# Pausing weight loads for DMA transposes, a by-token convolution mixer, and two 512-token tiles in a four-layer decoder trunk

## The chip, the cores and the metric

The kernel runs on the 8 cores of one Trainium2 chip, the same program on each, with no exchange between them. Each core has TensorE (PE) for matrix multiplies, whose results go to PSUM (8 banks of 512 float32 columns), VectorE (DVE), ScalarE (ACT), GpSimd (POOL) and SyncE (SP), the last two of which issue most transfers. The metric is the device time of the slowest core in microseconds (us).

## The reference, cut to what matters

Every core computes one prompt of 2048 tokens and 64 sample tokens through four layers. A layer is: a half-step SwiGLU feed-forward (FFN), a token mixer, and a second half-step FFN, each between two RMS norms.

```python
for i in range(4):
    f = swiglu(rmsnorm(h, g[0]), ffn_w_in[i, 0], ffn_w_down[i, 0])   # 1024 -> 2 x 2816 -> 1024
    h = h + 0.5 * rmsnorm(f, g[1])
    xm = rmsnorm(h, g[2])
    m = (conformer_conv, short_gated_conv, chunk_gmlp, multiscale_pool)[i](xm, ...)
    h = h + rmsnorm(m, g[3])
    f = swiglu(rmsnorm(h, g[4]), ffn_w_in[i, 1], ffn_w_down[i, 1])
    h = h + 0.5 * rmsnorm(f, g[5])
```

Mixer a (`conformer_conv`) projects to 2 x 1024 channels, gates (GLU), convolves each channel causally over 31 tokens, applies LayerNorm and swish, and projects out. Mixer b is a gated convolution of width 3, mixer c a chunked gMLP with GELU, a LayerNorm and a 128 x 128 position mixing, mixer d a causal pooling. Matrices are bfloat16 on TensorE, sums float32.

## The kernel before, in words

**A planner writes the program.** `build_program` runs generators (one for each chain of work) against a small model of the engines (`Prog`, `Sched`). Whenever its model of PE is free, `Sched.run` takes the ready request (`Pe`) with the smallest priority tuple and appends its matmuls to PE's stream; the other engines' streams grow the same way. The order on every engine is thus fixed at build time, and the chip keeps it whatever the real durations are. Semaphore waits are added for every true dependency.

**Work is tiled by tokens.** Two groups (`NG = 2`) pass one after the other through 11 stages each: group 0 has prompt tokens 0 to 1023 and the 64 sample tokens, group 1 has tokens 1024 to 2047. Stage number k counts 0 to 21; an FFN is one stage, a mixer one (mixer d is part of the chain after an FFN). A group's tokens are 8 `Tok` of 128 (taus 0 to 7; tau 8 is the samples). For matmuls whose moving operand is activations, they form three `NTile` of 384, 384 and 256 tokens (320 in group 0, with the samples).

**An FFN stage.** `ffn_in` multiplies, for each of 22 column blocks j of 128, gate and up: 8 matmuls (kc) each of a stationary 128x128 weight block against `xn[:, kc, nt.sl]`, for every NTile, in the order (q, jj, tile, gate/up) with j = 2q + jj. ACT evaluates Silu of the gate into a buffer `sg` (pool `P_SG`), DVE multiplies it with the up bank into `gb`. `ffn_down` (by `tok_mm`) multiplies tau by tau: 44 matmuls of 512 columns for a full tau, 11 weight slots (kb) in turn, all eleven needed by each tau.

**After each tau's last product** runs `chain`: `post` (square sum on ACT, power on POOL, two wide DVE operations) and `pre` (the same again for the next norm, one wide DVE operation into `xmb`, 3 buffers), and then the tau must be transposed into `xn`, channels on partitions, for stage k + 1. `pre` has two ways. By DMA: one transposing transfer on SP's queue. By PE: 8 transposes (line 84) into a bank and one copy out, on ACT as a rule. The DMA way is taken where `via == 'dma'` and the planner's model of POOL's queue would be empty within `LIGHT` = 4.0 us. That model takes 5 us for each weight load. Mixer a's chains say 'pe'; those of mixers b and c and of the FFNs say 'dma', and so fall to PE wherever the modelled queue is longer. The sample tau always goes by PE.

**Weights** stream through a ring of 16 slots of 4 KB per partition in one planned order (`build_plan`). `w_pump` issues the next load on POOL's queue as soon as a slot is free; a slot is freed (`w_free`) when every token tile has used it. Some slots are only lent as scratch ('lent': W, C, F for mixer a), with no load.

**Mixer a** (`mixer_a`): the in-projection has 8 channel blocks c, each for 3 NTiles, priority `(k, q // 2, nt.idx, c)`: c 0 to 3 for all tokens, then c 4 to 7 for all tokens. The convolution works on items (ct, hf): 256 tokens by four channel blocks, half hf, listed with all four hf = 0 items first. Each item first needs a shifted copy of its inputs in a buffer `xr` (2 buffers): `xr_load` issues 8 transfers on SP (16 for each of the 4 sample items of group 0) and makes 8 DVE copies. Then 128 matmuls with 32 stationary columns follow at priority `(k, -2, ...)`, ahead of everything else of the stage. When both halves of a ct are done, `stats` sums, normalises (DVE) and applies swish (ACT) into `xn`; then the out-projection of its taus, priority `(k, -1, ...)`, may run. The F slots hold the convolution's float32 results: six are lent, so hf = 0 items have their own slot each and hf = 1 items share two. The next FFN starts (`nextlane`) when the last main item is convolved, and goes beyond its column block 6 only when the sample items are done too.

**Mixer b** ends its in-projection with q = 3 and then has an out-projection of 8 (9) taus of 16 matmuls. **Mixer c** has v products tau by tau, u products by NTile, a position mixing (`splane`), and such an out-projection.

The ends of lines that readers of the profile meet: line 83 is any matmul, 84 a PE transpose, 85 an ACT activation, 86 to 89 DVE and POOL arithmetic, 242 any DMA issue.

Of the kernel before, what the change touches and what calls it, by code (L numbers as in the profile page):

```python
# [354 lines left out]


class Banks:
    def __init__(self, p):
# [171 lines left out]
def build_plan():  # L530
# [64 lines left out]
def build_program():  # L595
# [37 lines left out]
    with contextlib.ExitStack() as st:  # L633
# [47 lines left out]
        SG0 = A.reserve(4608)  # L681
        sg = [A.at(SG0 + i * 1536, [384], F32) for i in range(3)]
        h = A.alloc([9, D], F32)
# [8 lines left out]
        exts = A.at(o, [8, 34, 16], BF16); o += 8 * 34 * 16 * 2  # L692
        XR0 = o
        xr = [A.at(o + i * 16 * NXR * 2, [4, 4, NXR], BF16) for i in range(2)]
        xrs = [A.at(o + i * 16 * NXR * 2, [4, 2, 512], BF16) for i in range(2)]
        xrz = [A.at(o + i * 16 * NXR * 2, [8 * NXR], F32) for i in range(2)]
        o += 2 * 16 * NXR * 2
        glus2 = A.at(o, [8, NS], F32); o += 8 * NS * 4
        glus = A.at(o, [8, NS], F32); o += 8 * NS * 4
        gluf = A.at(XR0 - 8704, [8, 32], F32)  # L700
        assert o <= G0 + GSZ, (o - G0, GSZ)
# [19 lines left out]
        P_XMB = Pool(S, 'xmb', 3)  # L721
        P_SG = Pool(S, 'sg', 3)
        P_ZB = Pool(S, 'zb', 3)
# [3 lines left out]
        def grab(pool):  # L727
            while not pool.free:
                yield pool
            return pool.take()  # L730

        plan = []
# [7 lines left out]
        class WS:  # L740
            nxt = 0
            free = list(range(RING))
            slot = {}
            cap = 0

        def slot_off(k):
# [255 lines left out]
        def ffn_in(k, g_, l, s, nts, gate=None):  # L1002
            done = [Count(len(nts), lambda q=q: w_free((g_, 'fi', l, s, q, 0), (g_, 'fi', l, s, q, 1))) for q in range(NQ)]

            def ev(nt, j, up, bg, tg):
                n = nt.n
                yield p.t(tg)
                i = yield from grab(P_SG)
                ps, pid = bk(bg)
# [60 lines left out]
        def ffn_down(k, g_, l, s, taus, spawn):  # L1070
            yield from tok_mm(k, taus, lambda kc, t: gb[:, kc, t.sl],
                              lambda kb, t: [('g', k, t.n, 2 * kb), ('g', k, t.n, 2 * kb + 1)],
                              lambda kb, t: [('g', t.n, 2 * kb), ('g', t.n, 2 * kb + 1)],
                              [(g_, 'fd', l, s, kb) for kb in range(NQ)], NJ, spawn)

        XRI = [('xr', i, e) for i in range(2) for e in 'dv']

        def mixer_a(k, g_, nts, taus, nextlane):
            new = [('glub', n, c) for n in range(3) for c in range(8)] + ['glub_h', 'glub_p', 'exts_st', 'gluf'] + XRI + \
                  [(nm, c) for nm in ('exts', 'glus2', 'glus') for c in range(8)]  # L1080
            p.inherit(new, G_ALL)
            smp = g_ == 0
            last = g_ == NG - 1

            def init():
# [35 lines left out]
            def ev(c, nt, bg, tg):  # L1121
                n, np_ = nt.n, nt.npr
                yield p.t(tg)
                i = yield from grab(P_SG)
                ps, pid = bk(bg)
# [31 lines left out]
            def sub(nt):  # L1157
                n = nt.n
                for q in range(4):
                    kv, kg = (g_, 'ai', q, 0), (g_, 'ai', q, 1)  # L1160
                    for jj in range(2):
                        c = 2 * q + jj

                        def mm(b, key):
# [30 lines left out]
            NCT = GP // CT  # L1195
            items = [(ct, 0, None) for ct in range(NCT)] + [(ct, 1, None) for ct in range(NCT)]
            if smp:
                items += [('s', i // 2, i) for i in range(4)]

            def xr_load(i):  # L1200
                ct, hf, si = items[i]
                b = i % 2
                if ct == 's':
# [10 lines left out]
                else:  # L1214
# [14 lines left out]
                if i >= 2:  # L1229
                    yield Flag(('xfree', k, i - 2))  # L1230
                    yield p.rt_w([('xr', b, 'd'), ('xr', b, 'v')])
# [24 lines left out]
            def conv():  # L1256
                for i, (ct, hf, si) in enumerate(items):
                    n = CT if ct != 's' else NS
                    first = ct != 's' or si % 2 == 0
                    x = i % 2  # L1260
                    if ct != 's':
# [6 lines left out]
                    if first:  # L1268
                        fkey = 0 if ct == 's' else ct if hf == 0 else 4 + ct % 2
                        ids = [('fb', ct, c) for c in range(4 * hf, 4 * hf + 4)]  # L1270
                        if ct == 's':
                            p.inherit(ids, [('glus2', c) for c in range(4 * hf, 4 * hf + 4)])
                            off = None
                        elif hf == 1 and ct >= 2:
                            yield Flag(('lnd', k, ct - 2))
                            p.inherit(ids, [('fb', ct - 2, c) for c in range(4, 8)])
                            off = slot_off(PIDX[(g_, 'F', fkey)])
# [139 lines left out]
            def fclose(i):  # L1417
                yield Flag(('lnd', k, i))
                lent_close((g_, 'F', i), [('fb', i, c) for c in range(4)])
                if i >= 2:  # L1420
                    lent_close((g_, 'F', 2 + i), [('fb', ct, c) for ct in (i - 2, i) for c in range(4, 8)])
            for i in range(NCT):
                S.spawn(fclose(i))
# [8 lines left out]
        def mixer_b(k, g_, nts, taus, nextlane):  # L1432
# [13 lines left out]
            def ev(c, nt, b, tok):  # L1446
                n, np_ = nt.n, nt.npr
                yield p.t(tok)
                i = yield from grab(P_ZB)
                i2 = yield from grab(P_SG)  # L1450
                zk = zb[i]
# [46 lines left out]
            def sub(nt):  # L1498
                n = nt.n
                for q in range(4):  # L1500
                    for jj in range(2):
                        c = 2 * q + jj
                        for part, nm in ((2, 'bX'), (1, 'bC'), (0, 'bB')):
# [38 lines left out]
        def mixer_c(k, g_, nts, taus, nextlane):  # L1542
# [87 lines left out]
            def vlane(nt):  # L1630
                for t in nt.taus:
                    P = t.P
                    bb = None
                    for kb in range(4):
# [16 lines left out]
                        vcnt[kb].hit()  # L1651
                    S.spawn(v_ev(t, bb, tok))
                S.set(('vd', k, nt.idx))

            def sev(nt, hh, b, tok):
                n, np_ = nt.n, nt.npr
                yield p.t(tok)
                i = yield from grab(P_SG)
                ps, bid = bk(b)
# [49 lines left out]
            def after():  # L1709
                for nt in nts:  # L1710
                    yield Flag(('spd', k, nt.idx))
                if smp:
# [289 lines left out]
        for g_ in range(NG):  # L2002
            taus = [Tok(i, 128, i // 3 if i < 6 else 2) for i in range(8)]
            if g_ == 0:
                taus.append(Tok(8, 64, 2))
            nts = [NTile(0, 0, 384, 0, taus[0:3]), NTile(1, 384, 384, 0, taus[3:6]),
                   NTile(2, 768, 256, NS if g_ == 0 else 0, taus[6:])]
            groups.append((taus, nts))
        NSTG = 11
# [7 lines left out]
        def start(k, gate=None):  # L2017
            if k >= NSTG * NG:
                return
            g_, i = k // NSTG, k % NSTG  # L2020
            taus, nts = groups[g_]
            kind, l, s = KINDS[i]
# [123 lines left out]
```

How the kernel before makes its waits and increments, by code:

```python
    def _emit_waits(self, eng, deps):  # L158
        for sk in sorted(deps, key=str):
            v = deps[sk]
            if sk == ('e', eng) and eng in ('pe', 'sp'):
                continue
            if self.waited[eng].get(sk, 0) >= v:
                continue
            self.waited[eng][sk] = v
            sem = self.semh[sk]
            self.streams[eng].append(lambda e, sem=sem, v=v: e.wait_ge(sem, v))
# [37 lines left out]
    def op(self, eng, fns, reads=(), writes=(), cost=None):  # L205
        writes = list(writes) + [b for b in reads if isinstance(b, tuple) and b[0] == 'ps']
        deps = self._deps(reads, writes)
        self._emit_waits(eng, deps)
        if isinstance(fns, Fn):
            fns = [fns]
        if cost is None:
            cost = sum(f.cost(eng) for f in fns)
        start = self._start(eng, deps)
        self.efree[eng] = start + cost
        self.busy[eng] += cost
        self.ecount[eng] += 1
        c = self.ecount[eng]
        sem = self.semh[('e', eng)]
        for f in fns[:-1]:
            self.streams[eng].append(f)
        last = fns[-1]
        self.streams[eng].append(lambda e, last=last, sem=sem: last(e).then_inc(sem, 1))
        tok = (('e', eng), c)
        self.tend[tok] = start + cost + (0.17 if eng == 'pe' else 0.03)
        self._record(tok, reads, writes)
        return tok
```

## Time and profile before

| | us |
|---|---|
| median of 3 runs | 4662.27 (4657.13 to 4664.70) |
| the profiled execution, its own time | 4654.91 |
| its span, slowest core | 4653.4 (cores 4644.1 to 4653.4) |
| PE busy | 4566.7, 98% |
| DVE / ACT / POOL busy | 1770.4 / 1281.3 / 608.6 |
| share of PE in the chain that ended last | 92% |

The profile is one execution. Its page gives each engine's busy time and the costliest groups; a group is one line, engine and operation with its operands, the count behind an x, the busy time of the whole group, the mean duration of one instruction in ns, and the idle time of its engine ahead of it with what ended that. Matmuls overlap (a 384-column one is shown as 326 ns but the next starts 163 ns after it), so their pace is read from start to start. PEclk is the granted TensorE clock as a share of 2.4 GHz.

### The profile page before, as it was taken

The numbers are of one execution on the slowest core, as the hardware profiler recorded it, in microseconds if no ns is written. First come the engines' busy times: TensorE is split into PE (matmuls) and PEld (weight loads), VectorE is DVE, ScalarE is ACT, GpSimd is POOL, SyncE is SP. The second block draws the span as 40 slices with busy tenths as digits, with TensorE's granted clock in tenths as the row PEclk, the third lists the DMA queues.
The fourth block names the chain that finished last, engine by engine and source line by source line (L and its number), as shares of the span: only waits on it lengthen the run. The fifth ranks groups of instructions, "written<-read, shape, count | busy, mean of one in ns | idle before, by whom it ended". The sixth has DMA issues, their size and how long they took to land.

```text
span 4653.4 us, 83035 instructions; the slowest of 8 cores (4644.1 to 4653.4 us)
## 1 busy us (share of the span) xinstructions
PE 4566.7 (98%) x30474; PEld 2698.2 (58%) x30474; DVE 1770.4 (38%) x3156; ACT 1281.3 (28%) x2499; POOL 608.6 (13%) x1102
## 2 busy tenths in 40 slices
PE   7998999999999999999999989999999999999999
PEld 4555656556555565565646566565665655656564
DVE  2366232373232542326232472323723236232622
ACT  2135222233221331224121252222322225121421
POOL 1112110011010110102010111101101012010210
PEclk9998999999999999999999999999999999999999
DMA  8336527264263543635565246363543636444361
GB/s 167 68 73 124 103 53 137 48 117 85 55 111 62 106 84 61 118 60 93 98 139 98 63 90 112 57 118 57 105 92 57 117 57 123 73 80 98 60 119 41
DMA packets 228042, 416.39 MB, mean 89 GB/s; under 512 B 114095, under 2 KB 136879, under 8 KB 227630
## 3 DMA queue, kind: packets, MB, share of 16 engines
q0 software_dynamic: 88592, 319.79, 39.6%
q1 hardware_dynamic: 139054, 91.30, 8.0%
q8 instruction: 251, 4.11, 0.4%
q14 instruction: 145, 1.19, 0.1%
HBM read 682.92 MB, written 12.71 MB: 149 GB/s over the span
## 4 chain that ended last, share of the span: by engine, by line
PE 92%; DVE 2%; issue 2%; DMA 2%; SPq 1%; ACT 1%; POOL 0%; DVEq 0%; ACTq 0%; POOLq 0%
PE ps L83 91%; DVE big L88 1%; SPq L242 1%; PE ps L84 1%; ACT big L85 1%; DVE big L86 1%; DMA big<-wst 1%; DMA big<-big 1%; DMA big<-xp 0%; DVE big L89 0%; POOL big L86 0%; DVE big L87 0%; DVEq L167 0%; POOL big L242 0%; ACTq L167 0%
## 5 line engine op out<-in xcount | busy, mean ns | idle before, releaser
L83 PE MATMUL ps<-big 128*128 128x384 bf16 (+5 forms) x29758 | 4535.4, 322 | 47.6 <-DMA big<-big 13.3
L83 PEld LDWEIGHTS ps<-big 128*128 128x128 bf16 (+1 forms) x29758 | 2653.9, 99 | 1897.5 <-issue 137.4
L85 ACT ACTIVATE big<-ps 128x384 f32<-128x384 f32 (+5 forms) x1526 | 875.4, 577 | 2829.1 <-PE ps L83 2721.3
L86 DVE TENSOR_TENSOR big<-ps,big 128x384 bf16<-128x384 f32 (+6 forms) x1386 | 856.6, 618 | 1855.6 <-PE ps L83 1838.0
L88 DVE SCALAR_TENSOR_TENSOR big<-big 128x1024 bf16<-128x1024 f32 (+9 forms) x591 | 585.4, 995 | 184.0 <-POOL big L86 115.8
L242 POOL DMA_DIRECT2D big<-wst x608 | 327.2, 542 | 2456.3 <-PE ps L83 2296.4
L85 ACT ACTIVATE big<-big 128x1024 bf16<-128x1024 f32 (+5 forms) x454 | 344.4, 774 | 480.8 <-DVE big L88 308.7
L86 POOL TENSOR_TENSOR big<-big 128x1 f32<-128x1 f32 (+1 forms) x434 | 261.8, 605 | 1537.7 <-DVE big L87 1313.8
L87 DVE TENSOR_SCALAR big<-big 128x1 f32<-128x1 f32 (+2 forms) x439 | 78.6, 180 | 716.7 <-ACT big L85 703.2
L89 DVE COPY big<-big 32x1136 bf16<-32x1136 bf16 (+4 forms) x281 | 81.7, 291 | 19.5 <-ACT big L85 7.8
L84 PE MATMUL ps<-big 128*128 128x128 bf16 x716 | 57.5, 224 | 29.3 <-DVE big L88 18.1
L86 DVE TENSOR_TENSOR big<-big 128x384 bf16<-128x384 f32 (+13 forms) x120 | 78.9, 666 | 17.0 <-POOL big L91 9.3
L84 PEld LDWEIGHTS ps<-big 128*128 128x128 bf16 x716 | 47.8, 100 | 47.5 <-issue 37.9
L85 ACT ACTIVATE big<-ps,big 128x256 bf16<-128x256 f32 (+1 forms) x72 | 32.4, 453 | 45.6 <-PE ps L83 44.1
L87 DVE TENSOR_SCALAR big<-ps,big 128x256 f32<-128x256 f32 (+1 forms) x72 | 32.3, 459 | 32.7 <-ACT big L85 31.9
L85 ACT ACTIVATION_READ_ACCUMULATOR big<-ps 128x1 f32 x221 | 43.4, 196 | 0.0
L86 DVE TENSOR_TENSOR big<-big,ps 128x1024 f32<-128x1024 f32 (+1 forms) x36 | 40.6, 1129 | 2.9 <-PE ps L83 0.8
L85 ACT ACTIVATION_READ_ACCUMULATOR big<-big 128x1 f32 (+1 forms) x221 | 41.6, 188 | 0.0
L88 DVE SCALAR_TENSOR_TENSOR big<-ps,big 128x384 f32<-128x384 f32 (+2 forms) x64 | 31.2, 506 | 18.0 <-PE ps L83 13.1
L88 DVE SCALAR_TENSOR_TENSOR big<-big,ps 128x384 bf16<-128x384 f32 (+1 forms) x64 | 27.4, 432 | 25.0 <-PE ps L83 22.6
L91 POOL TENSOR_SCALAR_AFFINE_SELECT big<-big 128x64 bf16<-128x64 bf16 (+7 forms) x50 | 12.5, 257 | 42.4 <-DVE big L90 15.5
L85 ACT ACT_TABLE_LOAD x5 | 6.4, 1283 | 8.1 <-DMA big<-xp 5.9
(9 smaller groups left out, 20.5 us busy)
## 6 DMA issues: line engine op xcount, KB each, us to landing
big<-wst POOLq DMA_DIRECT2D x608, 512.0 KB, 8.4
big<-gains SPq DMA_DIRECT2D x52, 512.0 KB, 10.6
big<-xp SPq DMA_DIRECT2D x16, 512.0 KB, 5.1
yp<-big SPq DMA_DIRECT2D x16, 512.0 KB, 4.1
big<-big SPq DMA_DIRECT2D x64, 71.0 KB, 2.5
big<-big SPq DMA_DIRECT2D x64, 70.8 KB, 2.7
big<-big SPq DMA_DIRECT2D x48, 64.0 KB, 2.3
big<-dwx SPq DMA_DIRECT2D x4, 512.0 KB, 4.3
```

The lines of the kernel that those rows point to most:

```text
L83: 'matmul': lambda e, *a, **k: e.matmul(*a, **k),
L84: 'transpose': lambda e, *a, **k: e.transpose(*a, **k),
L85: 'activation': lambda e, *a, **k: e.activation(*a, **k),
L86: 'tensor_tensor': lambda e, *a, **k: e.tensor_tensor(*a, **k),
L87: 'tensor_scalar': lambda e, *a, **k: e.tensor_scalar(*a, **k),
L88: 'scalar_tensor_tensor': lambda e, *a, **k: e.scalar_tensor_tensor(*a, **k),
L89: 'tensor_copy': lambda e, *a, **k: e.tensor_copy(*a, **k),
L91: 'affine_select': lambda e, *a, **k: e.affine_select(*a, **k),
L242: self.streams[q].append(lambda e, out=out, in_=in_, sem=sem: e.dma_start(out=out, in_=in_).then_inc(sem, 16))
```

## The change

Three edits, in the diff below, in the order of its parts.

1. **The mixer a stage goes by tokens.** In-projection priority `(k, nt.idx, c, 0)`; items listed (ct 0, hf 0), (ct 0, hf 1), (ct 1, hf 0) and so on; three `xr` buffers in group 1 (the third lies where group 0 has its sample state), two in group 0; four F slots instead of six, of which ct 2 and 3 take those of ct 0 and 1 after these are normalised; the lent slots are planned after all eight in-projection loads instead of amid them; DVE copies of `xr_load` step back while DVE is busy (`polite`).
2. **Weight loads pause.** `w_hold(flag)` stops `w_pump` until a flag is set. Mixer b calls it after its last in-projection request, mixer c after its last v request; the flag is the last tau's `xn` for stage k + 1. Mixer c's chains say 'pe' for taus 0 to 2 and 'dma' for the others.
3. **Two tiles of 512 tokens** for `ffn_in` in group 1, in place of 384 + 384 + 256. The Silu buffers become two of 512 columns or three of 384 in the same bytes (`Widths`). Mixers keep three tiles.

```diff
+class Widths(Pool):
+    CLASH = {0: (3,), 1: (3, 4), 2: (4,), 3: (0, 1), 4: (1, 2)}
+    def take(self, wide):
+        c = [i for i in ((3, 4) if wide else (0, 1, 2)) if i not in self.busy and not any(x in self.busy for x in self.CLASH[i])]
...
-                        if q == 1:
-                            for i in range(4):
-                                lend(('W', i))
-                            for i in range(2):
-                                lend(('C', i))
-                            lend(('F', 0))
-                            lend(('F', 1))
-                    for i in range(2, 6):
+                    for i in range(2):
+                        lend(('W', 2 * i))
+                        lend(('W', 2 * i + 1))
+                        lend(('C', i))
+                        lend(('F', i))
+                    for i in range(2, 4):
                         lend(('F', i))
...
-            while WS.nxt < min(len(plan), WS.cap) and WS.free:
+            while WS.nxt < min(len(plan), WS.cap) and WS.free and not WS.held:
...
+        def w_hold(flag):
+            def rel():
+                yield Flag(flag)
+                WS.held = False
+                w_pump()
+            WS.held = True
+            S.spawn(rel())
...
-                for i in range(2):
+                for i in range(NX):
                     yield S.now + 1.0
                     p.op('pool', I.memset(xrz[i], 0.0), writes=[('xr', i, 'd'), ('xr', i, 'v')])
...
-                        pr = (k, q // 2, nt.idx, c)
+                        pr = (k, nt.idx, c, 0)
...
-            items = [(ct, 0, None) for ct in range(NCT)] + [(ct, 1, None) for ct in range(NCT)]
+            items = [(ct, hf, None) for ct in range(NCT) for hf in range(2)]
...
+                        yield from polite()
                         t2 = p.op('dve', fns, reads=rd, writes=[('xr', b, 'v')], cost=0.9)
...
-                        fkey = 0 if ct == 's' else ct if hf == 0 else 4 + ct % 2
+                        fkey = 0 if ct == 's' else 2 * (ct % 2) + hf
...
-                        elif hf == 1 and ct >= 2:
+                        elif ct >= 2:
                             yield Flag(('lnd', k, ct - 2))
...
+                    if q == 3 and nt is nts[-1]:
+                        w_hold(('xn', k + 1, taus[-1].idx))
...
+                    if t is taus[-1]:
+                        w_hold(('xn', k + 1, taus[-1].idx))
...
-                              [(g_, 'co', kb) for kb in range(4)], 8, lambda t, b: chain(k, t, b, False))
+                              [(g_, 'co', kb) for kb in range(4)], 8, lambda t, b: chain(k, t, b, False, 'pe' if t.idx < 3 else 'dma'))
...
+            ntf = nts
+            if g_ > 0:
+                ntf = [NTile(0, 0, 512, 0, taus[0:4]), NTile(1, 512, 512, 0, taus[4:8])]
...
-            ffn_in(k, g_, l, s, nts, gate)
+            ffn_in(k, g_, l, s, ntf, gate)
```

## Rows read from the trace of the kernel before

**Rows 1.** Page of the profile: engines' busy time, then the last chain by engine.

```profile
PE 4566.7 (98%) x30474; PEld 2698.2 (58%) x30474; DVE 1770.4 (38%) x3156; ACT 1281.3 (28%) x2499; POOL 608.6 (13%) x1102
...
PE 92%; DVE 2%; issue 2%; DMA 2%; SPq 1%; ACT 1%; POOL 0%; DVEq 0%; ACTq 0%; POOLq 0%
```

**Rows 2.** Stretches: us, busy of PE, PEld, DVE, ACT, POOL, PEclk, DMA share, GB/s.

```profile
280.80:364.80 84.00, 82.67 (x1130) 57.48 (x1132) 62.93 (x136) 34.58 (x89) 9.83 (x12) 1.00 0.51 95
364.80:470.00 105.20, 83.31 (x1071) 49.91 (x1071) 69.46 (x127) 58.66 (x128) 23.88 (x38) 0.87 0.73 133
...
2650.00:2736.80 86.80, 83.19 (x1249) 60.46 (x1247) 62.57 (x131) 33.80 (x78) 9.47 (x8) 1.00 0.44 96
2736.80:2801.00 64.20, 55.52 (x563) 33.40 (x563) 52.41 (x83) 44.44 (x85) 21.54 (x33) 0.92 0.65 112
```

**Rows 3.** PE in order of time, start, us, count, idle: stage 13's end to 14's.

```profile
3022.98 10.13 PE L83 MATMUL ps<-big 128*128 128x512 bf16 x60
...
3033.39 221.08 PE L83 MATMUL ps<-big 128*128 128x384 bf16 x1348
3254.31 0.61 PE L84 MATMUL ps<-big 128*128 128x128 bf16 x8
```

**Rows 4.** PE in order of time, end of mixer c in group 1.

```profile
3909.69 3.62 PE L83 MATMUL ps<-big 128*128 128x512 bf16 x16
3913.14 0.61 PE L84 MATMUL ps<-big 128*128 128x128 bf16 x8
3913.59 3.62 PE L83 MATMUL ps<-big 128*128 128x512 bf16 x16
...
3931.43 4.06 PE L83 MATMUL ps<-big 128*128 128x384 bf16 x24
3935.33 0.61 PE L84 MATMUL ps<-big 128*128 128x128 bf16 x8
```

**Rows 5.** Groups by form, 3030 to 3178: busy us, mean ns, idle before.

```profile
L83 PEld LDWEIGHTS ps<-big 128*128 128x128 bf16 x1008 | 97.1, 98 | 50.4 <-issue 3.9
L86 DVE TENSOR_TENSOR big<-ps,big 128x384 bf16<-128x384 f32 x42 | 23.4, 557 | 86.8 <-PE ps L83 86.8
L85 ACT ACTIVATE big<-ps 128x384 f32<-128x384 f32 x42 | 20.6, 491 | 82.8 <-PE ps L83 82.8
```

**Rows 6.** Groups by form, 3183 to 3252 (down-projection), weight loads of PE.

```profile
L83 PEld LDWEIGHTS ps<-big 128*128 128x128 bf16 x320 | 31.3, 98 | 37.8
```

**Rows 7.** Line 84 alone, from mixer b's and c's out-projections to the last transpose.

```profile
1030.00:1078.00 48.00, 4.65 (x60) 3.93 (x60) 1.00 0.55 95
1618.00:1673.00 55.00, 5.27 (x68) 4.47 (x68) 1.00 0.59 115
3342.00:3386.00 44.00, 4.87 (x64) 4.05 (x64) 1.00 0.50 101
3897.00:3943.00 46.00, 4.88 (x64) 4.18 (x64) 1.00 0.66 126
```

**Rows 8.** DMA issues of the page: count, KB each, median us to landing.

```profile
big<-wst POOLq DMA_DIRECT2D x608, 512.0 KB, 8.4
...
big<-big SPq DMA_TRANSPOSE x92, 3.1
```

**Rows 9.** POOL in order of time around mixer c's out-projection in group 1.

```profile
3888.59 0.53 POOL L242 DMA_DIRECT2D big<-wst  x1 [0.29 <-issue]
...
3925.68 1.10 POOL L242 DMA_DIRECT2D big<-wst  x2
```

**Rows 10.** GB/s in 40 slices of 3342 to 3386 (1.1 us each).

```profile
GB/s 0 15 67 186 220 201 216 201 223 123 0 0 0 0 0 0 7 7 0 0 0 0 0 0 0 15 0 0 134 175 175 186 227 194 223 272 276 283 216 190
```

**Rows 11.** What PE waited for, 364 to 470: us, times, longest.

```profile
PE ps L83 <- DMA big<-big: 13.3, 4, 6.6
```

**Rows 12.** SP's queue in order of time, 350 to 450: start, us, what.

```profile
356.02 11.47 SPq L242 DMA_DIRECT2D big<-big  x16
```

**Rows 13.** The chain that ended last, 364 to 470: start, us, what.

```profile
366.85 16.73 DMA big<-big
```

More of the change, by code:

```diff
@@ L354, in give, with __init__ @@
             self.S.push(self.S.now, self.waiters.pop(0))
+class Widths(Pool):
+    CLASH = {0: (3,), 1: (3, 4), 2: (4,), 3: (0, 1), 4: (1, 2)}
+    def __init__(self, S, name):
+        Pool.__init__(self, S, name, 0)
+        self.busy = set()
+    def take(self, wide):
+        c = [i for i in ((3, 4) if wide else (0, 1, 2)) if i not in self.busy and not any(x in self.busy for x in self.CLASH[i])]
+        if not c:
+            return None
+        k = min(c, key=lambda i: self.S.p.rt_w([(self.name, x) for x in (i,) + self.CLASH[i]]))
+        self.S.p.inherit([(self.name, k)], [(self.name, x) for x in self.CLASH[k]])
+        self.busy.add(k)
+        return k
+    def give(self, k):
+        self.busy.remove(k)
+        w, self.waiters = self.waiters, []
+        for g in w:
+            self.S.push(self.S.now, g)
 class Banks:
@@ L681, in build_program @@
         SG0 = A.reserve(4608)
-        sg = [A.at(SG0 + i * 1536, [384], F32) for i in range(3)]
+        sg = [A.at(SG0 + i * 1536, [384], F32) for i in range(3)] + [A.at(SG0 + i * 2560, [512], F32) for i in range(2)]
         h = A.alloc([9, D], F32)
@@ L692, in build_program @@
         exts = A.at(o, [8, 34, 16], BF16); o += 8 * 34 * 16 * 2
[L693 to L697, printed above, removed]
         glus2 = A.at(o, [8, NS], F32); o += 8 * NS * 4
         glus = A.at(o, [8, NS], F32); o += 8 * NS * 4
-        gluf = A.at(XR0 - 8704, [8, 32], F32)
+        gluf = A.at(o - 1024, [8, 32], F32)
+        XRO = [o, o + 32 * NXR, G0 + 8 * (32 + GP) * 2]
+        assert XRO[2] + 32 * NXR <= o - 1024
+        xr = [A.at(x, [4, 4, NXR], BF16) for x in XRO]
+        xrs = [A.at(x, [4, 2, 512], BF16) for x in XRO]
+        xrz = [A.at(x, [8 * NXR], F32) for x in XRO]
+        o += 2 * 32 * NXR
         assert o <= G0 + GSZ, (o - G0, GSZ)
@@ L721, in build_program @@
         P_XMB = Pool(S, 'xmb', 3)
-        P_SG = Pool(S, 'sg', 3)
+        P_SG = Widths(S, 'sg')
         P_ZB = Pool(S, 'zb', 3)
@@ L730, in grab, with polite, grab_sg @@
             return pool.take()
+        def polite(eng='dve'):
+            while p.efree[eng] > S.now + 0.25:
+                yield p.efree[eng] - 0.15
+        def grab_sg(n):
+            while True:
+                k = P_SG.take(n > 384)
+                if k is not None:
+                    return k
+                yield P_SG
         plan = []
@@ L744, in build_program @@
             cap = 0
+            held = False
         def slot_off(k):
@@ L1007, in ev @@
                 yield p.t(tg)
-                i = yield from grab(P_SG)
+                i = yield from grab_sg(n)
                 ps, pid = bk(bg)
@@ L1071, in ffn_down @@
             yield from tok_mm(k, taus, lambda kc, t: gb[:, kc, t.sl],
-                              lambda kb, t: [('g', k, t.n, 2 * kb), ('g', k, t.n, 2 * kb + 1)],
-                              lambda kb, t: [('g', t.n, 2 * kb), ('g', t.n, 2 * kb + 1)],
+                              lambda kb, t: [('g', k, t.nf, 2 * kb), ('g', k, t.nf, 2 * kb + 1)],
+                              lambda kb, t: [('g', t.nf, 2 * kb), ('g', t.nf, 2 * kb + 1)],
                               [(g_, 'fd', l, s, kb) for kb in range(NQ)], NJ, spawn)
-        XRI = [('xr', i, e) for i in range(2) for e in 'dv']
+        XRI = [('xr', i, e) for i in range(3) for e in 'dv']
         def mixer_a(k, g_, nts, taus, nextlane):
@@ L1082, in mixer_a @@
             smp = g_ == 0
+            NX = 2 if smp else 3
             last = g_ == NG - 1
@@ L1123, in ev @@
                 yield p.t(tg)
-                i = yield from grab(P_SG)
+                i = yield from grab_sg(n)
                 ps, pid = bk(bg)
@@ L1201, in xr_load @@
                 ct, hf, si = items[i]
-                b = i % 2
+                b = i % NX
                 if ct == 's':
@@ L1228, in piece @@
                                 glub[32 * q:32 * q + 32, 4 * hf:4 * hf + 4, t0 + s_:t0 + s_ + w])
-                if i >= 2:
-                    yield Flag(('xfree', k, i - 2))
+                if i >= NX:
+                    yield Flag(('xfree', k, i - NX))
                     yield p.rt_w([('xr', b, 'd'), ('xr', b, 'v')])
@@ L1259, in conv @@
                     first = ct != 's' or si % 2 == 0
-                    x = i % 2
+                    x = i % NX
                     if ct != 's':
@@ L1273, in conv @@
                             off = None
-                        elif hf == 1 and ct >= 2:
+                        elif ct >= 2:
                             yield Flag(('lnd', k, ct - 2))
-                            p.inherit(ids, [('fb', ct - 2, c) for c in range(4, 8)])
+                            p.inherit(ids, [('fb', ct - 2, c) for c in range(4 * hf, 4 * hf + 4)])
                             off = slot_off(PIDX[(g_, 'F', fkey)])
@@ L1418, in fclose @@
                 yield Flag(('lnd', k, i))
[L1419 to L1422, printed above, removed]
+                for hf in range(2):
+                    lent_close((g_, 'F', 2 * (i % 2) + hf), [('fb', ct, c) for ct in (i - 2, i) for c in range(4 * hf, 4 * hf + 4)])
+            for i in range(2, NCT):
                 S.spawn(fclose(i))
@@ L1449, in ev @@
                 i = yield from grab(P_ZB)
-                i2 = yield from grab(P_SG)
+                i2 = yield from grab_sg(n)
                 zk = zb[i]
@@ L1657, in sev @@
                 yield p.t(tok)
-                i = yield from grab(P_SG)
+                i = yield from grab_sg(n)
                 ps, bid = bk(b)
@@ L2007, in build_program @@
                    NTile(2, 768, 256, NS if g_ == 0 else 0, taus[6:])]
-            groups.append((taus, nts))
+            ntf = nts
+            if g_ > 0:
+                ntf = [NTile(0, 0, 512, 0, taus[0:4]), NTile(1, 512, 512, 0, taus[4:8])]
+            for n in ntf:
+                for t in n.taus:
+                    t.nf = n.idx
+            groups.append((taus, nts, ntf))
         NSTG = 11
@@ L2020, in start @@
             g_, i = k // NSTG, k % NSTG
-            taus, nts = groups[g_]
+            taus, nts, ntf = groups[g_]
             kind, l, s = KINDS[i]
```

## The prediction

> **What bounds the kernel now.** I read the page first: PE is busy 98% of the span and makes up 92% of the chain that ended last, DVE 38%, ACT 28% [rows 1]. So time can only come from three places: PE's idle time (4653.4 - 4566.7 = 87 us), stretches at half clock, and matmul time itself. Next I read the table of stretches, to see where the first two lie. Both mixer a stages stand out [rows 2]. Group 0 spends 189.2 us there with PE idle 1.3 + 21.9 = 23.2 us, and a granted clock of 0.87 over 105.2 us, which is 13.7 us of lost clock; group 1 spends 151 us with 3.6 + 8.7 = 12.3 us idle and 0.08 x 64.2 = 5.1 us of lost clock. Together 54 us. The clock is at its upper level (2.4 GHz) before PE begins to wait and falls to the lower one within the waits. Third, I read PE in order of time, start to start, for the pace of each form. A run of 16 down-projection matmuls of 512 columns takes 3.45 us, 0.2156 us each; 24 matmuls of 384 columns take 3.90 us, 0.1625 us each; 8 transposes 0.45 us [rows 4].
>
> **Part 3, two tiles of 512.** Between two transposes lie 221 us without a gap: 3033.39 to 3254.31 is 220.92 us for 1348 matmuls [rows 3]. The run of 60 matmuls at 3022.98 begins with the last 4 of stage 13's down-projection, so 56 of stage 14's 1056 in-projection matmuls (704 of 384 columns, 352 of 256) are in it, all of 384. The long run thus has 648 of 384, 352 of 256 and 348 of 512 columns. 348 x 0.2156 = 75.0 and 648 x 0.1625 = 105.3, so the 352 small ones cost 40.6 us, 0.115 us each, where 256 columns at 2.4 GHz are 0.107 us. The in-projection costs 105.3 + 9.1 (the 56) + 40.6 = 155.0 us; with 704 matmuls of 512 columns it costs 704 x 0.2156 = 151.8 us. The saving is 3.2 us in each of 8 FFN stages of group 1: **25 us**.
>
> Where it comes from matters, since a fixed cost for each matmul would not give so much. The weight loads of the in-projection show 3.9 us of idle time put down to "issue" in 148 us; in the down-projection none [rows 5, 6]. I read it so: at a change of bank PE's queue holds a semaphore wait ahead of the next weight load (98 ns), and a 256-column matmul is too short to cover both, one of 512 is not. It is about once per block j. The lower end: the wait stays visible behind 512 columns and only the rest of the difference remains, 25 - 8 x 22 x 0.1 = 8 us. The upper end is the 25.
>
> The Trainium skill (TensorE: Matmul & The Clock Gate, "Wait — 56ns, not 53.3ns?") gives the warm start-to-start time as N / 2.4 GHz plus about 2.5 ns. By that rule alone three tiles made two save one such cost in 352 x 8 places, an estimate of 7 us in place of 25. The trace agrees with it for 384 and 512 columns and not for 256.
>
> Other engines: Silu of 384 columns is 491 ns and the product 557 ns [rows 5]; by proportion 512 columns are at most 655 and 743 ns. A gate and up pair then takes PE 3.45 us, and an `sg` buffer is held from the gate's end to the product's, about 1.73 + 0.9 = 2.6 us. Two buffers suffice; DVE is a third busy. At a stage's start tile 0 now needs tau 3 too. In the FFN after mixer c the transposes of taus 0 to 3 come during the last four out-projection taus, so tau 3 may be late by its landing, 1 to 2 us; where an FFN or a mixer b went before, it is early. I take 0, range 0 to 5 us for all. Tile 0 alone has 76 us of products to cover the chains of taus 4 to 7.
>
> **Part 2, the pause.** Transposes by PE around the four out-projections of mixers b and c: 60, 68, 64 and 64, in 4.9 us or so each [rows 7]. That is 7 full taus and the half-size sample tau (4), then 8 and that, 8, 8. A DMA transpose lands in 3.1 us [rows 8]. The choice hangs on the planner's queue: at mixer b's tau 0 it still holds the loads that the last in-projection block frees, 3 x 5 us modelled; the pause leaves these out, and the queue falls under 4 us. I expect 7 + 8 taus of mixer b and taus 3 to 7 of mixer c twice: 25 taus, 25 x 0.45 = **11 us** of PE, and 25 copies of ACT. Lower end 3 us (mixer c's five of one group and little else), upper end 14 us (with small waits of PE ahead of transposes). The latency is about equal: 3.1 us against 0.45 plus a copy plus the wait for a slot on PE.
>
> What queues behind the pause is POOL's weight loads. In group 1 the loads of 3888 and on, which mixer c's v and u slots free, and those of 3925 [rows 9] all wait for tau 7's `xn` at about 3942. At that point at least 4 slots hold q 0 and 1 of the next FFN, probably 6. Tile 0 alone uses q 0 and 1 in 13.8 us from 3927, so PE has work until 3941, then tile 1 becomes ready and has the same again until 3955. Real loads under a backlog move 190 to 230 GB/s [rows 10], 2.3 to 2.8 us for a slot of 0.52 MB; q 2 lands by 3950. I take 0; 0 to 3 us for each mixer c, nothing for mixer b, whose ring holds about nine slots of the next FFN. The debt of ten slots is repaid at 2.8 us a slot against a use of 6.9.
>
> **Part 1, mixer a by tokens.** The matmuls stay. What changes is what is ready when PE would wait. Now, after the last in-projection product (364.8 and 2736.8), five (in group 1 six) of eight main items are convolved, and the rest, LayerNorm and all eight out-projection taus hang on one another. PE waited 13.3 us for `xr` transfers in group 0, longest 6.6 [rows 11]; the transfer before the next item took 16.7 us, among five weight loads [rows 13], where an item's 8 issues take 8 x 11.47 / 16 = 5.7 us of SP [rows 12]. By tokens, ct 0 is done a third through the projection and its LayerNorm and two out-projection taus fit under the rest. Against it: eight in-projection weights and eight lent slots fill the ring of 16, and the weights are freed only by the last token tile. So F 2 and 3, and with them ct 1, wait for c 1 of tile 2, and `ao` for c 3 to 5. From there (T) SP needs for group 1's items 5 to 7, with three buffers, about 25 us; PE has 10.5 us of in-projection, six items of 3.7 us (22 us) and two ready out-projection taus (7 us): 39 us. So the transfers are covered. After item 7 LayerNorm takes about 15 us, against which stand four out-projection taus (14 us) and the next FFN's first tile. I expect group 1 to keep 4 of 12 us of idle and 2 of 5 of clock: -11. In group 0 SP needs about 31 us for items 4 to 7 and then 4 x 11.5 = 46 us for the sample items, unchanged by the order, and cover runs out there as now. Of the 37 us there I take 7 off. Sum **-18 us**. Bounds: -45 (nearly all of 54 gone), and +15 (the tail of out-projections is used up early, and PE waits for 17 us landings once more in each group).
>
> **Sum.** 25 + 11 + 18 = 54 us less; I add 3 for the small waits above: -51 us, so 4654.9 - 51 = 4604 for an execution like the profiled one. The median of the runs shown is 7.4 us above that execution: 4662.3 - 51 = **4611 us**.
>
> **Rivals.** (a) Mixer a gains nothing: what the tail saves by being shorter it loses by having less to fill it, since out-projection taus run as soon as they are ready. For it: the ring is full until the last tile, and SP's sample items do not move. Then -36 + 3: 4629. (b) The wait at the bank change is not hidden by 512 columns, or the saving is of fixed costs alone (the page's rule): 8 us in place of 25, 4628. Against it: no idle time before weight loads in the down-projection [rows 6]. (c) The pause doesn't do what it says (the modelled queue is still too long for most taus), or costs as much as it gives by late weights after mixer c: 11 us less gain, 4622. (d) Slower: **mixer a's items become bound by landings**. If each of the six items after T waits for a transfer of 17 us (the row of group 0) and the samples follow, group 0 has 6 x 17 + 46 + 15 = 163 us from T, group 1 117 us. Now the tails after the projection are 105 and 64 us [rows 2], and T lies about 25 us before the projection ends, items in between included. That is 33 and 28 us longer, all of it idle, partly at half clock: +61, less 36, +3 for late starts: 4690. It decides from 36 us of growth over both stages. Against it: only one of eight items landed so late, among five weight loads at once, and by tokens these loads come two at a time. (e) Mixer a's waits go nearly all, -45: 4584.
>
> **How the numbers follow.** Forecast 0.50, (a) 0.22, (b) 0.08, (c) 0.08, (d) 0.05, (e) 0.07. The predicted time is the forecast's. The low end takes in half of (e) and the bounds of parts 2 and 3 (another 3 us): 4588. The high end takes in (a) to (c) and a wait of 10 us on top of (a): 4640. What this kernel's measurement can tell from no change is about 0.2%, 9 us. Faster by more: all but (d) and mixes of (a), (b) and (c), 0.90; within, 0.05; slower, 0.05.
>
> **What would show it.** Right: an FFN in-projection of group 1 at 151.8 us without a 384- or 256-column matmul and no "issue" idle before its weight loads; about 516 transposes on line 84 in place of 716 and 117 DMA transposes for 92; 2816 fewer in-projection matmuls; POOL without a weight load from mixer b's last product until tau 7 or 8 is transposed; mixer a stretches with less idle and a clock above 0.92. Wrong: PE idle ahead of the first 512-column matmuls of an FFN, waits for `wst` after a pause, or mixer a stretches longer than 189 and 151 us.

## The result

The changed kernel is slower: 4691.3 us median (4686.7 to 4693.4) against 4660.0 for the kernel before, ratio 1.0065 with a 95% interval of 1.0049 to 1.0080. The forecast was 4611 us, the range 4588 to 4640, so the sign was wrong too: 0.7% slower, where 1.1% faster was forecast. The profiled execution took 4693.4 us. Some executions, whatever the kernel, show a lower granted clock on one die and are slower; all numbers here are without them, but a milder case of the kernel before, beside e1 to e4 (4712.2 us), and one of e5 (4776.5 us) are in the ratios, so the intervals of e1, e2, e4 and e5 are wide.

Its page, in the lines that answer to [rows 1] and [rows 8] (busy time by engine, the chain's shares), and the PE groups and the weight loads' issues:

```profile
PE 4535.0 (97%) x27466; PEld 2425.7 (52%) x27466; DVE 1743.5 (37%) x2983; ACT 1226.2 (26%) x2296; POOL 606.0 (13%) x1103
...
PE 91%; DMA 3%; DVE 2%; issue 2%; ACT 1%; SPq 0%; POOL 0%; DVEq 0%; ACTq 0%; POOLq 0%
...
L83 PE MATMUL ps<-big 128*128 128x512 bf16 (+9 forms) x26942 | 4510.9, 338 | 122.6 <-DMA big<-big 94.2
...
L84 PE MATMUL ps<-big 128*128 128x128 bf16 x524 | 43.0, 226 | 25.0 <-DVE big L88 17.4
...
big<-wst POOLq DMA_DIRECT2D x608, 512.0 KB, 8.7
```

PE does less, 4535 us in place of 4567, and yet the span is 38 us longer: its idle time went from 87 to 157 us, and 94.2 of that was ended by a transfer within SBUF. The transposing transfers, all of them (count; duration of the issue; to landing, min/median/max):

```profile
L240 SPq DMA_TRANSPOSE big<-big x116: 1216/1217/9127, 234.5 to 4432.4; - x116
...
  PE ps L83: 90.2, 6
...
DMA to landing us min/median/max: 3.0/3.1/34.4
```

The median is the 3.1 us of [rows 8]; the maximum is 34.4. To find where, I compared the stages of the two traces. The four FFNs that follow mixers b and c stand out. Stretches of the kernel before (us, busy of PE, PEld, DVE, ACT, POOL, granted clock, DMA share, GB/s):

```profile
1062.00:1306.90 244.90, 244.90 (x1482) 141.53 (x1480) 75.81 (x123) 55.28 (x108) 28.94 (x51) 1.00 0.37 69
1651.40:1898.10 246.70, 245.76 (x1499) 142.52 (x1497) 78.10 (x126) 59.37 (x113) 30.00 (x54) 1.00 0.37 69
3372.90:3606.20 233.30, 232.94 (x1442) 137.95 (x1440) 69.13 (x110) 53.23 (x105) 28.46 (x52) 1.00 0.39 75
3927.00:4161.90 234.90, 233.63 (x1450) 138.27 (x1449) 70.30 (x112) 55.55 (x108) 29.15 (x53) 1.00 0.39 74
```

and the same four stages of the changed kernel:

```profile
1038.30:1301.80 263.50, 245.77 (x1459) 141.06 (x1458) 76.92 (x125) 52.86 (x107) 30.67 (x56) 0.97 0.43 75
1644.70:1917.70 273.00, 246.89 (x1459) 141.17 (x1458) 77.58 (x126) 54.64 (x109) 33.06 (x61) 0.95 0.48 79
3380.40:3630.90 250.50, 230.97 (x1065) 104.32 (x1066) 66.08 (x90) 46.24 (x79) 31.52 (x57) 0.96 0.46 80
3948.90:4207.00 258.10, 231.77 (x1065) 104.46 (x1066) 66.26 (x90) 47.15 (x80) 33.04 (x60) 0.95 0.48 84
```

PE is idle for 17.7 + 26.1 + 19.5 + 26.3 = 90 us in them, where it was 2.6 us, and they are 85 us longer. All other stages together are 47 us shorter; 18 us of part 1, 3 us of part 3 in each of the six other FFNs of group 1, and 11 us of transposes that PE no longer does would make that up (an estimate).

**One of the four, step by step.** After mixer b in group 1. PE, SP and POOL of the changed kernel in order of time (start, us, what, idle before):

```profile
3380.42 19.15 PE L83 MATMUL ps<-big 128*128 128x512 bf16 x88 [1.34 <-DMA big<-big]
3419.08 6.09 PE L83 MATMUL ps<-big 128*128 128x512 bf16 x17 [19.51 <-DMA big<-big]
```

```profile
3389.24 1.10 SPq L242 DMA_DIRECT2D big<-gains  x2
3390.43 9.13 SPq L240 DMA_TRANSPOSE big<-big  x1
```

```profile
3387.99 0.55 POOL L86 TENSOR_TENSOR big<-big 128x1 f32<-128x1 f32 x1 [1.95 <-DVE big L87]
3388.55 1.64 POOL L242 DMA_DIRECT2D big<-wst  x3
3392.59 2.20 POOL L242 DMA_DIRECT2D big<-wst  x4 [2.40 <-issue]
```

The small POOL operation at 3387.99 is the power of tau 7's last norm. The weight loads that the pause held back stand right behind it in POOL's stream, and go out at 3388.55, **before** SP issues tau 7's transpose at 3390.43. The reader can see why in the diff: `w_hold` keeps the planner from *appending* the loads until its modelled time of tau 7's `xn`; it adds no semaphore. On the chip their only conditions are free slots. The kernel before issues the first three of these seven loads at 3343.29, when the in-projection ends, and the other four from 3370.62 to 3374.45, when the out-projection's last products free their slots; the pause makes one burst of them. So POOL runs ahead, and the transpose, which must land before the second 512-token tile may start, meets seven loads. It landed 28.4 us after its issue, at 3418.8. PE had 19.15 us of matmuls that don't need it, then stood still for 19.5 us. In the kernel before, the test against `LIGHT` had kept DMA transposes away from loads: the slowest of its 92 landed in 5.6 us. The pause makes the modelled queue look empty, so the test passes, while the real queue is about to fill.

**Why so long.** The transfers in flight, by queue (packets, MB, share of 16 engines), first of the changed kernel between 3404 and 3416, then of the kernel before around one transpose that has the engines for itself:

```profile
q0 software_dynamic: 570, 2.07, 96.7%
q1 hardware_dynamic: 571, 0.15, 9.3%
```

```profile
DMA packets 1056, 0.26 MB, mean 87 GB/s; under 512 B 1056, under 2 KB 1056, under 8 KB 1056
...
big<-big SPq DMA_TRANSPOSE x1, 3.1
```

A transpose is 1056 packets of 256 bytes. The weight loads' packets are fourteen times as large (2.07 MB / 570 = 3.6 KB). In 12 us each queue moved the same number, 571 and 570. I read it so: one packet of each goes in turn, so beside a backlog each small packet costs a large one's time. The Trainium skill says so (DMA: Bandwidth & Descriptors, "Queues, rings and completion order"): an engine goes round the queues that have work, one packet at a time. The trace agrees, with 571 against 570, and shows the price for a transfer made of small packets.

### The profile page after: what moved, and what is told of

The parts are those of the page before. It is cut to its first block, busy times and chain, and to the rows that moved or that the text cites. A ratio compares the mean times of both kernels' runs of the same rounds, so it can differ in the third digit from the quotient of the medians.

```text
span 4691.8 us, 75452 instructions; the slowest of 8 cores (4665.4 to 4691.8 us)
## 1 busy us (share of the span) xinstructions
PE 4535.0 (97%) x27466; PEld 2425.7 (52%) x27466; DVE 1743.5 (37%) x2983; ACT 1226.2 (26%) x2296; POOL 606.0 (13%) x1103
## 4 chain that ended last, share of the span: by engine, by line
PE 91%; DMA 3%; DVE 2%; issue 2%; ACT 1%; SPq 0%; POOL 0%; DVEq 0%; ACTq 0%; POOLq 0%
PE ps L83 91%; DMA big<-big 3%; DVE big L88 1%; ACT big L85 1%; DVE big L86 1%; PE ps L84 1%; SPq L242 0%; DVE big L89 0%; DMA big<-wst 0%; POOL big L86 0%; DVEq L167 0%; DMA big<-xp 0%; DVE big L87 0%; ACT L85 0%; POOL big L242 0%
## 5 line engine op out<-in xcount | busy, mean ns | idle before, releaser
L83 PE MATMUL ps<-big 128*128 128x512 bf16 (+9 forms) x26942 | 4510.9, 338 | 122.6 <-DMA big<-big 94.2
L83 PEld LDWEIGHTS ps<-big 128*128 128x128 bf16 (+3 forms) x26942 | 2392.6, 99 | 2217.2 <-issue 178.6
L85 ACT ACTIVATE big<-ps 128x384 f32<-128x384 f32 (+7 forms) x1327 | 822.4, 623 | 2918.5 <-PE ps L83 2819.2
L86 DVE TENSOR_TENSOR big<-ps,big 128x384 bf16<-128x384 f32 (+6 forms) x1210 | 828.7, 685 | 1940.6 <-PE ps L83 1923.9
L85 ACT ACTIVATE big<-big 128x1024 bf16<-128x1024 f32 (+7 forms) x450 | 343.1, 777 | 491.4 <-DVE big L88 322.0
L89 DVE COPY big<-big 32x1136 bf16<-32x1136 bf16 (+3 forms) x281 | 84.0, 299 | 19.6 <-ACT big L85 7.4
L84 PE MATMUL ps<-big 128*128 128x128 bf16 x524 | 43.0, 226 | 25.0 <-DVE big L88 17.4
L84 PEld LDWEIGHTS ps<-big 128*128 128x128 bf16 x524 | 35.4, 101 | 39.1 <-issue 30.9
L90 POOL MEMSET big<- 128x2272 f32 (+1 forms) x6 | 10.1, 1691 | 4.0 <-PE ps L83 3.7
```

What stands on the lines that cost most here:

```text
L83: 'matmul': lambda e, *a, **k: e.matmul(*a, **k),
L84: 'transpose': lambda e, *a, **k: e.transpose(*a, **k),
L85: 'activation': lambda e, *a, **k: e.activation(*a, **k),
L86: 'tensor_tensor': lambda e, *a, **k: e.tensor_tensor(*a, **k),
L89: 'tensor_copy': lambda e, *a, **k: e.tensor_copy(*a, **k),
L90: 'memset': lambda e, *a, **k: e.memset(*a, **k),
```

## The experiments

**Theory L (late landing):** the above, and nothing else in the change costs time. **Rival W:** the pause starves PE of weights. **Rival T:** DMA transposes every 3.5 us slow one another. All three leave PE waiting at the same place. The kernel before, run again beside them, took 4655.8 to 4663.6 us, and once the 4712.2 us named above. The times of e3 and e8 are of one execution each.

### e1: tau 7 by PE

```diff
-lambda t, b: chain(k, t, b, False, 'pe' if t.idx < 3 else 'dma'))
+lambda t, b: chain(k, t, b, False, 'pe' if t.idx < 3 or t.idx == 7 else 'dma'))   # mixer c
-lambda t, b: chain(k, t, b, False))
+lambda t, b: chain(k, t, b, False, 'pe' if t.idx == 7 else 'dma'))                # mixer b
```

> The changed kernel, but tau 7 after mixers b and c is transposed on PE (line 84) instead of by a DMA; all else is the same, the pause and its burst of 7 to 10 weight loads too. Theory L (late landing: the loads held back by the planner are held by no semaphore, so POOL issues them at once, ahead of tau 7's transposing transfer, which then lands with the last of them, 25 to 34 us later): the four waits of 17.7, 26.1, 20.9 and 26.9 us go, 84 to 90 us in all, 32 more transposes on line 84 cost 2 us: 4600 to 4612 us. Rival W (the pause starves PE of weights: the first 512-column products wait for the loads themselves): the waits stay, now put down to the weight loads, 4680 to 4695. Rival T (a row of DMA transposes every 3.5 us is what makes them slow): tau 6's would be late in its place, over 15 us to landing, 4670 or so.

Measured: 4608.5 to 4611.3 us, 82 us less than the changed kernel; ratio to the kernel before 0.9866 (0.978 to 0.9952). T and W fall: tau 6's transpose, now the last by DMA, landed in 8.1 us at most, and waits for weights are 1.8 us. The burst still goes out; in group 1 tau 6 meets its beginning. What PE waited for in e1 (us in total, times, longest), for transfers within SBUF:

```profile
PE ps L83 <- DMA big<-big: 8.8, 4, 3.7
```

### e2 and e9: a true wait

```diff
                 WS.held = False
-                w_pump()
+                w_pump([('xn', i, c) for i in range(8) for c in range(8)])
```

`w_pump` passes the list as reads, so POOL waits for the transposes' semaphores ahead of the first load.

> The changed kernel with a true wait: the first weight load after a pause waits on POOL for the landing of all taus' transposes. Theory L: tau 7's transfer lands in 3 to 4 us as the others do, the loads follow it, and come early enough (q 2 of the next FFN is needed some 14 us after tile 1 begins): 4600 to 4612 us, within 5 us of the run with tau 7 on PE. Rival W: PE now waits for weights after the pause, 5 to 15 us at each of the four places, put down to the weight loads: 4625 to 4660.

> The kernel of e2 once more, for its interval: parts 1, 2 and 3 with the true wait. Parts 1 and 3 gave 24 and 25 us alone and 50 together; the true pause adds 25 fewer PE transposes, 11 us at most: 4598 to 4604 us, ratio 0.987.

Measured: 4597.7 to 4604.3 us in e2, ratio 0.9847 (0.973 to 0.9965); 4600.9 to 4602.4 us in e9, ratio 0.9872 (0.9852 to 0.9891). The loads now follow the landing, which is 5.8 us after the issue at 3344.15; SP's and POOL's queues of e2 at the same place, then PE:

```profile
3344.15 1.25 SPq L240 DMA_TRANSPOSE big<-big  x1
```

```profile
3341.71 0.55 POOL L86 TENSOR_TENSOR big<-big 128x1 f32<-128x1 f32 x1 [1.59 <-DVE big L87]
3350.58 1.64 POOL L242 DMA_DIRECT2D big<-wst  x3 [8.33 <-PE ps L83]
```

```profile
3334.49 40.74 PE L83 MATMUL ps<-big 128*128 128x512 bf16 x188 [1.35 <-DMA big<-big]
```

(The wait is put down to PE, long done; a wait for several semaphores is put down badly where one is a transfer's.) POOL stands 8.3 us and PE runs through. All 114 transposes of e2 land in 3.0 to 6.1 us (e9: to 7.5), and waits of PE for weights are 3.3 us in the whole kernel: W is refuted for the pause itself. e2 also answers a rival that I had not named: two transfers of gains, 512 KB each, stand right ahead of tau 7's transpose on SP's own queue in all four places. They do so in e2 too, and by themselves they leave it at 6.1 us or less.

### e3: two loads ahead of the transpose

```diff
-                w_pump()
+                keep, WS.cap = WS.cap, WS.nxt + 2
+                w_pump()
+                WS.cap = keep
+                w_pump([('xn', i, c) for i in range(8) for c in range(8)])
```

> The changed kernel, with two weight loads let go at the end of the pause as now, and the others made to wait for the landing of the transposes. Theory L, by dose: 7 loads ahead gave 25.6 and 28.4 us to landing, 10 gave 33.7 and 34.4, so about 2.8 us each and a share for the first; two give 8 to 12 us to landing, and PE waits for them 0 to 3 us in each place: 4603 to 4620 us. If landing took a fixed 25 us whatever is ahead (something else than the queue), it stays at 25 us or more and the time at 4680.

Measured: 4619.1 us, in the expected 4603 to 4620. The dose, tau 7's time to landing: two loads ahead 12.0, 8.5, 13.3 and 14.5 us, seven 25.6 and 28.4, ten 33.7 and 34.4 (in the first of these two places the last two loads went out just behind the transpose); about 2.7 us for each load, and no fixed 25 us. Two of the four lie above the 8 to 12 us of the expectation and one at its end. That expectation left out the two gains transfers; they begin 1.2 and 2.3 us ahead of the transpose where it took 13.3 and 14.5 us, and 5.6 and 4.6 us ahead where it took 12.0 and 8.5, which fits, but no run takes them away. What PE waited for in e3 (us in total, times, longest):

```profile
PE ps L83 <- DMA big<-big: 20.5, 7, 5.5
```

### e4 to e7: the parts one by one

e4 drops both calls of `w_hold` and mixer c's 'pe' from the changed kernel. e5 adds only these to the kernel before. e6 is the kernel before with `ntf` and the wide `sg` buffers, e7 with mixer a's part alone.

> The changed kernel without its pause (no hold, mixer c's chains say dma for all taus as before): parts 1 and 3 alone. By the stages of the two traces part 3 gives 3.0 us in each of 8 stages and part 1 about 19 us, nearly all in group 0: 4617 us (4611 to 4625). If part of the loss were in the new tiles or in the order of mixer a, it would be above 4630.

> The kernel before with part 2 alone (the pause, mixer c's chains as changed). Theory L: 25 fewer PE transposes give 11 us, four late landings of tau 7 cost 75 to 90 us; with three tiles in group 1 the FFN's last tile (taus 6 and 7) alone waits, and tiles 0 and 1 cover a few us more than the one 512-token tile does: 4715 to 4740 us, against 4660. The rival, that the loss needs the new tiles or mixer a's order beside the pause: 4650.

> The kernel before with part 3 alone (two 512-token tiles in group 1's FFNs). 3.0 us in each of 8 stages and nothing else: 4636 us, ratio 0.9948. If only the fixed cost of each matmul were saved: 4652.

> The kernel before with part 1 alone (mixer a by tokens). The stages of the two traces give 19 us in group 0 and about 0 to 5 in group 1: 4638 us (4632 to 4645). If mixer a gained nothing: 4660.

| kernel | parts | median us | ratio (95%) | against before beside it |
|---|---|---|---|---|
| e5 | 2 | 4735.0 | 1.0186 (1.0144 to 1.0227) | +77 |
| e6 | 3 | 4634.1 | 0.9947 (0.9927 to 0.9967) | -24 |
| e7 | 1 | 4633.6 | 0.9944 (0.9924 to 0.9964) | -25 |
| e4 | 1, 3 | 4608.4 | 0.9861 (0.9776 to 0.9947) | -52 |
| changed | 1, 2, 3 | 4691.3 | 1.0065 (1.0049 to 1.0080) | +31 |
| e2 | 1, 2 with a true wait, 3 | 4597.9 | 0.9847 (0.973 to 0.9965) | -63 |
| e9 | the same | 4601.4 | 0.9872 (0.9852 to 0.9891) | -60 |

The last column is the difference of medians; the ratios go by means, and e5's holds its 4776.5 us, without which it would be 1.016.

The parts add up: 77 - 24 - 25 = +28 against +31 measured. The pause alone is the loss; in e5, too, the tiles and mixer a being as before, PE waits for transfers within SBUF (us in total, times, longest):

```profile
PE ps L83 <- DMA big<-big: 97.6, 7, 24.8
```

e4 against e2 and e9 is what part 2 is worth if it does what it says: 4605.3 to 4609.4 against 4597.7 to 4604.3, 1 to 12 us, so its size is not well fixed; the medians are 7 to 10 us apart. e2 has 23 transposes more by DMA than e4 (114 against 91), which at 0.45 us each is 10 us of PE.

### e8: is a 256-column matmul slow by itself?

e8 is e6 with a third tile.

```diff
-ntf = [NTile(0, 0, 512, 0, taus[0:4]), NTile(1, 512, 512, 0, taus[4:8])]
+ntf = [NTile(0, 0, 512, 0, taus[0:4]), NTile(1, 512, 256, 0, taus[4:6]), NTile(2, 768, 256, 0, taus[6:8])]
```

> Part 3 alone, but with FFN tiles of 512, 256 and 256 tokens in group 1. Theory S (a semaphore wait at the gate-to-up bank change costs 0.1 us behind a 256-column matmul and nothing behind a longer one): one more small tile per block j, so 44 such waits a stage in place of the 22 of the kernel before: a steady in-projection of 352 x (0.216 + 2 x 0.109) + 44 x 0.1 = 157 us where the kernel before has 155 and the changed one 152; about 2 x 21 x 0.19 = 8 us of issue idle ahead of the weight loads in 150 us. Rival F (a 256-column matmul is slow by itself, 0.115 us each): 352 x (0.216 + 0.230) = 157 us as well, but no more issue idle than before. Whole kernel: 4675 us.

Measured: 4676.5 us in one execution, 18 above the kernel before, as both theories had it. They differ in the weight loads. PE's weight loads in an in-projection, of e8 and then of the changed kernel (count, busy us, mean ns, idle before and what ended it):

```profile
L83 PEld LDWEIGHTS ps<-big 128*128 128x128 bf16 x988 | 94.5, 98 | 52.9 <-issue 6.1
```

```profile
L83 PEld LDWEIGHTS ps<-big 128*128 128x128 bf16 x675 | 66.0, 98 | 79.4
```

With one small tile a block there are 3.9 us of issue idle [rows 5], with two 6.1, with none none. More small tiles bring more such waits, against rival F, though 6.1 is less than the 8 of theory S. PE itself now shows 1.4 us of idle before 256-column matmuls. I take the wait at the bank change as supported, not as measured one by one.

### e10: the pause over FFNs too

```diff
+                        if hold and ti == len(taus) - 1:
+                            w_hold(('xn', k + 1, t.idx))
...
+hold=(l, s) in ((0, 1), (1, 1), (2, 1))
```

> The kernel of e2 with the truly waiting pause also over the last tau of the FFNs that another FFN follows (layer 0 second, layer 1 second, layer 2 second), so that their taus 6 and 7 go by DMA too: 114 planned DMA transposes become 120, 6 x 0.45 = 2.7 us less on PE. The loads of 11 slots come about 20 us later. If they land in 2.5 to 3 us each as the traces show, nothing waits for them: 4595 to 4600. Rival: the next FFN's third weight block comes too late once in each place, 2 to 5 us: 4600 to 4625.

Measured: 4598.5 us median (4596.0 to 4601.8), ratio 0.9866 (0.9849 to 0.9883), beside e9's 0.9872 (0.9852 to 0.9891). 120 DMA transposes and 492 on line 84 are the 6 taus moved; PE's waits for weights are 0.5 us. Its median is the lowest but for e2's, and the step from e9 is within the measurement. The rival's late weight block is not seen.

## Why the prediction was wrong, point by point

**The step that failed** is in part 2: "The loads of 3888 and on ... and those of 3925 all wait for tau 7's `xn` at about 3942." They wait in the planner only. I had written in the kernel's description that the order on each engine is fixed at build time, and did not draw the conclusion that order within one queue says nothing about another: POOL and SP run free of each other between semaphores. I asked whether the loads come too late, priced that at 0 to 6 us, and never asked whether they come too early. Of the signs that I had listed, "PE idle ahead of the first 512-column matmuls of an FFN" came true. "The latency is about equal: 3.1 us" took a landing from stretches without loads. A row for the other case was at hand: a transfer of 16.7 us among five weight loads [rows 13]. I used it to price mixer a, rival (d), and not the transpose that the change moves next to such a burst. The term measured 90 us of PE idle in the four FFNs, 87 more than before, where the sum had 0 to 3 for each mixer c and nothing for b.

**What the pause did otherwise.** 116 DMA transposes in place of 92, 524 on line 84 in place of 716: 24 taus moved, 25 forecast. At the four out-projections 56 are left of the 256 in [rows 7], which is the 25; elsewhere one tau more goes by PE. With a true wait that is worth 1 to 12 us (e4 against e2); 11 forecast.

**Part 3** was right: 25 us forecast, 24 measured alone (e6). The in-projection of stage 14 and its down-projection in the changed kernel, in order of time:

```profile
3044.94 218.59 PE L83 MATMUL ps<-big 128*128 128x512 bf16 x1012
3263.36 0.61 PE L84 MATMUL ps<-big 128*128 128x128 bf16 x8
```

3263.36 - 3044.94 = 218.4 us for 1012 matmuls is 0.2158 us each, and 704 of them 151.9 us; forecast 151.8. Rival (b) falls: 24 us were saved and not 8. The prediction's estimate of 7 us by the rule of the Trainium skill (TensorE: Matmul & The Clock Gate, "Wait — 56ns, not 53.3ns?") is not borne out for the tile of 256 columns; for 512 columns the trace agrees with it, with 0.2158 us. Two `sg` buffers sufficed: the 1012 matmuls run without a gap. Why 256 columns cost 0.115 us stays supported by e8 and not shown.

**Part 1** was right in sum and wrong in place: 18 forecast; measured alone (e7) 25 by the medians and 18 by the spans of the profiled executions (4635.2 against 4653.4). The stretches that answer to [rows 2] in the changed kernel:

```profile
278.60:374.00 95.40, 90.74 (x1271) 63.25 (x1270) 73.82 (x151) 44.25 (x109) 10.21 (x12) 0.97 0.51 101
374.00:463.00 89.00, 85.14 (x1015) 50.94 (x1014) 63.32 (x119) 51.75 (x111) 22.31 (x36) 0.97 0.68 129
2664.10:2752.20 88.10, 83.28 (x1129) 60.31 (x1127) 64.23 (x125) 35.34 (x81) 10.65 (x11) 0.96 0.40 77
2752.20:2816.00 63.80, 54.96 (x661) 32.62 (x662) 51.76 (x89) 40.47 (x77) 15.36 (x26) 0.97 0.66 107
```

In group 0 idle time fell from 23.2 to 8.5 us and the clock in the tail rose from 0.87 to 0.97; PE's 13.3 us of waits for `xr` transfers [rows 11] are gone. I had forecast 7 us there. My SP times of 25 and 31 us for three and four items don't follow from the 5.7 us an item given beside them (17 and 23 us). In group 1, where I had forecast 11, idle time is 13.7 us against 12.3: the tail did not shrink. The stages tell the same: mixer a and the FFN behind it are 19 us shorter in group 0 and only 2 us in group 1, where part 3 alone gives 3. The waits there changed hands. The kernel before waited for DVE (line 86, 3.9 us) and ACT (3.4 us); the changed one waits for transfers within SBUF (4.0 us), for DVE (line 89, 3.0 us) and for weights (1.9 us). Why they are as long in sum stays open.

**The rivals.** The measured time, 4691, is that of rival (d), 4690, by accident: it put the loss into mixer a, whose stages took 184.4 us in place of 189.2 in group 0 and 151.9 in place of 151.0 in group 1. Of rival (c), that the pause doesn't do what it says, I priced the two ways that cost 11 us; the third, that the loads are not held at all, was missing. The low end, 4588, does not follow from its own terms either: half of (e) and 3 us give 4594. The chance of 0.05 for slower was too small since it came from one mechanism, and the part with a hold across two queues had no rival that could cost more than it gives.

## What to carry to other kernels

A scheduler that decides *when to append* an instruction has decided nothing about when the chip runs it. For each step that must come after another on a different queue, name the semaphore; if there is none, ask what happens when the queue runs as far ahead as its true dependencies allow, too early as well as too late. Before a transfer is put next to others, price it with a row from a stretch that has them, and weigh its packets: a transfer of 256-byte packets pays a large packet's time for each when it shares the engines.

## What the runs showed of the hardware that I had not expected

Behind seven loads of 0.5 MB a 0.26 MB transpose lands with the last of them (28.4 us in place of 3.1); in 12 us of this the two queues moved 571 and 570 packets, but 0.15 and 2.07 MB. Its issue on SP took 9.1 us in place of 1.2, so whatever stands behind it on that queue is late too. The wait also costs clock. The changed kernel before, in and after the wait of 19.5 us (columns as in the stretches above):

```profile
3380.40:3399.50 19.10, 19.08 (x88) 8.50 (x88) 11.03 (x16) 6.32 (x11) 6.85 (x11) 1.00 0.72 122
3399.50:3419.00 19.50, 0.07 (x1) 0.00 (x0) 0.00 (x0) 0.60 (x1) 0.00 (x0) 0.59 0.97 178
3419.00:3425.00 6.00, 5.92 (x17) 2.23 (x18) 0.00 (x0) 0.60 (x1) 0.00 (x0) 0.61 0.01 3
3425.00:3431.00 6.00, 6.00 (x29) 2.74 (x28) 1.38 (x2) 1.19 (x2) 1.07 (x2) 1.00 0.41 48
```

The granted clock is 0.59 in the wait and 0.61 in the 6 us after it, mostly the 1.2 GHz level, and then 1.00 again: 17 matmuls took 5.9 us where 17 x 0.2158 = 3.7 would do. So this wait cost about 2 us more than its idle time. After the other three waits the granted clock of the 6 us that follow is 0.64, 0.51 and 0.51, 2 to 3 us each.
